# Delta rule: the inverse is turned by TensorE at each doubling level, in place of a transposed copy kept with its own products

## What is computed

```python
a_mat = jnp.where(strict, jnp.einsum('bnhid,bnhjd->bnhij', kb, kc) * decay, 0.0)
t_mat = lax.linalg.triangular_solve(a_mat, eye, left_side=True, lower=True, unit_diagonal=True)
u = jnp.einsum('bnhij,bnhjd->bnhid', t_mat, vc * bc[..., None])
w = jnp.einsum('bnhij,bnhjd->bnhid', t_mat, kb * jnp.exp(gc)[..., None])
```

## Time and profile before

| | |
|---|---|
| median of 3 runs | 2700.0 us (2696.96 to 2703.47) |
| span of the profiled execution | 2699.0 us |
| PE busy | 2646.7 us, 98% of the span |
| PEld busy | 2419.6 us, 90% |
| DVE busy | 1835.7 us, 68% |
| ACT busy | 1007.2 us, 37% |
| POOL busy | 344.1 us, 13% |
| moved by DMA | 398.75 MB, mean 148 GB/s |

### The profile page before, as it was taken

The page is one execution under the profiler, slowest core; times in us unless marked ns, Lnnn a source line. Parts: engine busy times, 40 slices in busy tenths (PEclk is TensorE's granted clock), DMA queues, the critical chain, the costliest instruction groups (busy, mean ns, idle before and its releaser), DMA issues.

```text
span 2699.0 us, 44506 instructions
## 1 busy us (share of the span) xinstructions
PE 2646.7 (98%) x17640; PEld 2419.6 (90%) x17640; DVE 1835.7 (68%) x1775; ACT 1007.2 (37%) x1045; POOL 344.1 (13%) x350
## 2 busy tenths in 40 slices
PE   8999999999999999999998999999999999999998
PEld 7999988888888987878888999999999998788886
DVE  4444545555554233548889888888888888888898
ACT  4443322222222232223354444444444444333334
POOL 5000044444442420101000000000000000000000
PEclk9999999999999999999999999999999999999999
DMA  4333222222223433679524445444544459866562
GB/s 138 102 88 91 79 79 79 82 81 78 78 78 86 109 94 117 221 268 319 187 103 133 150 161 171 155 152 148 179 148 155 151 172 305 292 205 203 175 196 104
DMA packets 345656, 398.75 MB, mean 148 GB/s; under 512 B 11481, under 2 KB 300386, under 8 KB 344418
## 3 DMA queue, kind: packets, MB, share of 16 engines
q1 hardware_dynamic: 285970, 333.30, 39.3%
q10 hardware_dynamic: 59616, 64.49, 7.0%
HBM read 325.92 MB, written 71.83 MB: 147 GB/s over the span
## 4 chain that ended last, share of the span: by engine, by line
PE 91%; DVE 2%; issue 2%; DMA 2%; ACT 1%; SPq 1%; POOL 1%; DVEq 0%; ACTq 0%; POOLq 0%
PE psum L2082 33%; PE psum L2399 10%; PE psum L2401 10%; PE psum L2400 10%; PE psum L2374 6%; PE psum L2375 6%; PE psum L2376 6%; PE psum L2242 2%; PE psum L2237 1%; DMA w_raw<-in_w_proj_a 1%; PE psum L2031 1%; PE psum L2059 1%; DMA dn_raw<-in_w_ffn_down 1%; PE psum L2221 1%; PE psum L2314 1%
## 5 line engine op out<-in xcount | busy, mean ns | idle before, releaser
L2082 PE MATMUL psum<-hn_hi,w_hi 128*128 128x264 f32 (+1 forms) x1600 | 450.7, 330 | 0.0
L2082 PE MATMUL psum<-hn_lo,w_hi 128*128 128x264 f32 (+1 forms) x1600 | 449.9, 330 | 0.0
L2082 PE MATMUL psum<-hn_hi,w_lo 128*128 128x264 f32 (+1 forms) x1600 | 449.9, 330 | 0.0
L1347 DVE TENSOR_TENSOR w_lo<-w_raw,w_hi 128x1024 fp32r<-128x1024 f32 x144 | 186.6, 1297 | 253.5 <-ACT w_hi L901 253.0
L901 ACT ACTIVATE w_hi<-w_raw 128x1024 fp32r<-128x1024 f32 x144 | 152.1, 1057 | 373.7 <-PE psum L2082 345.5
L2082 PEld LDWEIGHTS psum<-hn_lo,w_hi 128*128 128x128 f32 x1600 | 269.1, 188 | 22.7 <-issue 0.7
L2082 PEld LDWEIGHTS psum<-hn_hi,w_lo 128*128 128x128 f32 x1600 | 268.9, 188 | 22.4
L2082 PEld LDWEIGHTS psum<-hn_hi,w_hi 128*128 128x128 f32 x1600 | 269.1, 188 | 22.0 <-issue 0.2
L2374 PE MATMUL psum<-dn_hi,act_hl 128*128 128x512 f32 x616 | 240.2, 390 | 4.3 <-DVE hq L1684 2.5
L2376 PE MATMUL psum<-dn_hi,act_hl 128*128 128x512 f32 x616 | 239.8, 389 | 0.0
L2375 PE MATMUL psum<-dn_lo,act_hl 128*128 128x512 f32 x616 | 239.8, 389 | 0.0
(11 more groups left out here) (355 smaller groups left out, 6400.5 us busy)
## 6 DMA issues: line engine op xcount, KB each, us to landing
w_raw<-in_w_in SPq DMA_DIRECT2D x144, 512.0 KB, 3.9
ffn_raw<-in_w_ffn_gate SPq DMA_DIRECT2D x44, 1024.0 KB, 6.5
ffn_raw<-in_w_ffn_up SPq DMA_DIRECT2D x44, 1024.0 KB, 6.7
dn_raw<-in_w_ffn_down SPq DMA_DIRECT2D x32, 1024.0 KB, 8.3
act_hl<-act_dram SPq DMA_DIRECT2D x56, 512.0 KB, 9.0
act_dram<-comb_hi ACTq DMA_DIRECT2D x22, 896.0 KB, 4.2
act_dram<-comb_lo ACTq DMA_DIRECT2D x22, 896.0 KB, 6.2
out_raw<-in_w_out SPq DMA_DIRECT2D x16, 1024.0 KB, 9.8
```

The costliest lines, as they stand in the source:

```text
L1347: dve.tensor_tensor(wlo[s][:], raw[s][:], whi[s][:].bitcast(F32), ALU.subtract).then_inc(S["lo_ready"], 1)
L2082: ins = pe.matmul(o, lhs, r, start=kt == 0 and i == 0, stop=kt == 4 * n_chunks - 1 and i == 2)
```

## The change

V, its copy, its products and its subtractions go. At each of the first six levels, after DVE has made the new `Z`, PE turns it (four transposes of 128x128 against the identity, into bank 2), and DVE multiplies bank 2 with the mask to give the next `X`. Within a level Z's product now comes first and the turn second. The number of steps on PE and of pieces on DVE and ACT stays as it was; so does the place of the weight splits among them. POOL's program is not edited.

```diff
@@ ACT, gdn_act
-                act.wait_ge(S["x_ready"], LEVELS * v + 1)
-                act.activation(B[1][:], bank(0), ACT.Copy).then_inc(S["v_copied"], 1)
@@ DVE, gdn_dve
                 for l in range(LEVELS):
-                    if l < LEVELS - 1:
-
-                        dve.wait_ge(S["v_copied"], v + 1)
-                        dve.wait_ge(S["vx_product"], (LEVELS - 1) * v + l + 1)
-                        v_even = blocks_of(B[1][:], l, 0)
-                        dve.tensor_tensor(v_even, v_even, blocks_of(bank(2), l, 0), ALU.subtract).then_inc(S["v_ready"], 1)
-                        dve.wait_ge(S["v_ready"], (LEVELS - 1) * v + l + 1)
-                        dve.wait_ge(S["mask_ready"], LEVELS * v + l + 2)
-                        if l >= 1:
-                            dve.wait_ge(S["z_product"], LEVELS * v + l)
-                        dve.tensor_tensor(XB[(l + 1) % 2][:], B[1][:], mask_buf[(l + 1) % 2][:], ALU.mult) \
-                            .then_inc(S["x_ready"], 1)
-                        yield
                     dve.wait_ge(S["z_kept"], LEVELS * v + l + 1)
                     dve.wait_ge(S["z_product"], LEVELS * v + l + 1)
                     dve.tensor_tensor(B[11][:], kept[:], bank(1), ALU.subtract).then_inc(S["z_ready"], 1)
                     yield
+                    if l < LEVELS - 1:
+                        dve.wait_ge(S["z_turned"], (LEVELS - 1) * v + l + 1)
+                        dve.wait_ge(S["mask_ready"], LEVELS * v + l + 2)
+                        dve.tensor_tensor(XB[(l + 1) % 2][:], bank(2), mask_buf[(l + 1) % 2][:], ALU.mult) \
+                            .then_inc(S["x_ready"], 1)
+                        yield
@@ PE, gdn_pe
                     pe.wait_ge(S["x_ready"], LEVELS * v + l + 1)
                     pe.wait_ge(S["z_ready"], (LEVELS + 1) * v + l + 1)
-                    if l < LEVELS - 1:
-                        for i in range(GH):
-                            ins = pe.matmul(blocks_of(bank(2), l, 0)[:, i, :, :], B[11][:, i, :],
-                                            blocks_of(x[:], l, 0)[:, i, :, :], start=True, stop=True)
-                        ins.then_inc(S["vx_product"], 1)
-                        yield
                     for i in range(GH):
                         ins = pe.matmul(bank(1)[:, i, :], x[:, i, :], B[11][:, i, :], start=True, stop=True)
                     ins.then_inc(S["z_product"], 1)
                     yield
+                    if l < LEVELS - 1:
+                        pe.wait_ge(S["z_ready"], (LEVELS + 1) * v + l + 2)
+                        for i in range(GH):
+                            ins = pe.transpose(bank(2)[:, i, :], B[11][:, i, :], ident[:])
+                        ins.then_inc(S["z_turned"], 1)
+                        yield
```

More of the change, by code:

```diff
@@ L130 @@
 nbeg_ready beta_k_ready vb_ready kd_factor kd_ready kk_done kq_done nt_ready pt_ready s_products rhs_ready
-qs_ready n_turned z_masked z_ready z_kept z_product mask_ready x_ready v_copied v_ready vx_product vn_product
+qs_ready n_turned z_masked z_ready z_kept z_product mask_ready x_ready z_turned vn_product
 vn_ready o_product ds_product o_ready state_ready o_squared o_sum o_mean o_rms o_scaled o_turned o_stored
@@ L446, in heads_of @@
             return v.unsqueeze(2).broadcast_to([P, GH, width])
-        def blocks_of(b, l, odd):
-            return b.rearrange("p h (n two s) -> p h n two s", two=2, s=1 << l)[:, :, :, odd, :]
         def over_heads(m):
```

## The result

| | before | after |
|---|---|---|
| median of the runs | 2698.74 us (4 runs) | 2677.44 us (4 runs) |
| span of the profiled execution | 2699.0 us | 2678.8 us |

The ratio is 0.992, 95% interval 0.9907 to 0.9932: 21.3 us less by the medians, 20.2 us by the two profiled spans. The forecast was 2678 us.

What follows compares the result with a forecast made beforehand. The prediction took PE, busy almost without waits, to bound the stage. 48 cheaper steps save 21.6 us and stalls cost 0: span 2699.0 - 21.6 = 2677.4 us, median 1.0 us above, so 2678 us; range 2672 to 2687.

Steps and rivals of the forecast that it cites:

- What bounds the stage: 331 to 866 us: PE busy for 531.68 of 535 us, one wait of 3.3 us, so time taken from PE is saved.
- The price of a step: PE, 48 steps: V's product at 1.35 us replaced by a turn at 0.91; 0.45 us a step taken, 21.6 us in all.
- The turn's wait for Z: PE's turn waits for DVE's new Z, ready 0.88 us before the step is due; nothing new to pay.
- Z's product's wait for X: PE in each level: X ready 1.42 us after the turn, Z's product due at 2.29; cover 0.87 us, no stall.
- piece 11: DVE's weight split ahead of the fourth X: fits by 0.3 us; 0 taken, 0 to 5.6 us possible in seven half-chunks.
- POOL's late kept product: POOL at level 3: mask, copies and `kept` move back, cover 1.2 us; priced 0, other end 3.5 us in seven half-chunks.
- The sum: Whole kernel: span 2699.0 - 21.6 + 0 = 2677.4 us; median 1.0 us above the span, so 2678 us.
- A: Rival, every level: Z's product waits for X, the hand-off becomes the bound; 34.6 us of stall, 2713 us; chance 2%.
- C: Rival: the tight places, piece 11 and the late `kept`, stall by 5.6 and 3.5 us, 2687 us; chance 12%.
- B: Rival, PE in the levels: extra transposes let the clock fall to 1.2 GHz; 2941 us at worst; chance 2%.
- D: Rival, behind the stage: a later stage waits for a transfer and the gain is given back, 2700 us; chance 2%.
- E: Rival, PE's step: the turn costs as much as a product, 1.35 for 1.35 us, 2700 us; chance 2%.

Runs made afterwards that it cites:

- the turn as a product: The changed kernel with the turn written as an ordinary product of Z with the identity, eight instructions a step: 2700.05 us, ratio 0.9999 to the kernel before.
- the work put back: The changed kernel with a DVE subtraction after each X and ACT's copy of bank 0 once a half-chunk put back: 2678.60 us, ratio 0.9925.
- the wide version: The kernel before with V's product over all 128 columns of each head instead of 64: 2700.12 us, ratio 0.9998.
- The two late versions: The changed kernel with one or two extra 128x512 DVE operations ahead of each X: 2676.93 us (ratio 0.9915) and 2702.68 us (1.0013).
- the version without it: The changed kernel with DVE's weight split of piece 11 moved behind the next piece, the fourth X: 2678.00 us, ratio 0.9922, period 62.97 us.

## Why the prediction was right

- **What bounds the stage.** Right. PE without a wait in the rows meant that its steps are the time; the turn as a product and the work put back show it from both sides.
- **The price of a step.** Right: 1.35 us against 0.90, where 0.91 and 0.44 to 0.46 us of difference were read from the turn of N. The reading that columns don't set the price of V's product is confirmed by the wide version. The turn costs the same on Z as on N.
- **The turn's wait for Z and Z's product's wait for X.** Right at five levels of six: X 0.73 us after the turn and 0.69 us long, 0.87 us ahead of the matmuls, to the hundredth of what the rows gave. But the prediction counted the cover to the matmuls, and the weight loads, which stand behind the wait, begin 0.23 us earlier. The cover that counts is 0.64 us, and the 0.3 us that it gave piece 11 were 5.02 - 0.23 - 4.73 = 0.06. The two late versions bracket the cover between 0.61 and 1.22 us.
- **Piece 11.** Here a term was mis-sized: 0 was taken, with 0 to 5.6 us as its bounds, and the weight loads wait 3.0 us in all, of which the periods show 0.19 us a half-chunk, 1.5 us. The step that failed is the split's length: 1.59 us was taken over from the kernel before, where the split ran beside POOL's copies. It begins 2.53 us into the step (which starts at 433.00), where the rows gave 2.52, but takes 1.96 us, and X is done 5.10 us into it and not 4.73. What it runs beside had changed, though POOL's program was not edited. The copies begin 0.19 us into the step, where 0.3 was forecast, but take 1.72 us and not 3.18, so the kept product begins 2.13 us into it, 0.4 us ahead of the split. By the forecast it would have begun at about 3.7 us, behind the split's start. The prediction moved POOL's operations and kept the durations that they and the split had in other company.
- **POOL's late kept product.** Right in that nobody waits for it; wrong in the duration of the copies ahead of it, below.
- **The sum.** 21.6 us were forecast; 20.1 us come from the periods, and the difference is the 1.5 us of piece 11, by the version without it. That the median, 2677.44 us, lies within 1 us of the forecast is luck: the sum is 1.5 us off, and the four runs lie between 2675.60 and 2680.62 us.
- **The rivals.** A, the hand-off as the bound, was not so, but it lies close: two more DVE operations bring the time back to that of before. Of C a part came. B did not come: the granted clock is 1.00 over six half-chunks, each with 11 groups of four transposes where there were five. The Trainium skill, page "TensorE: Matmul & The Clock Gate", Part 4, says that the full clock does not engage for transposes; beside these gate matmuls the measurement says otherwise, and it decides. D and E fell with the time behind the last mark and with the rows of the turn.

## What to carry to other kernels

Where TensorE is without gaps, price its steps by the distances between starts. For the small products here these went with the number of instructions and not with columns: a transposition of an operand that is at hand can be cheaper than a product that updates a copy of it. Then look at what the shorter way takes away elsewhere: here the slack of an operand fell from 2.55 us to 0.87 (0.64 to the weight loads, which is where the wait stands), and one operation of another engine that ran 0.37 us longer than forecast was enough for a wait. And when a dependence moves, lay out the whole new order of an engine that was not edited, with what it runs beside, not only whether it is in time.

## What the runs showed of the hardware

- A 128x512 turn in float32 is four instructions and holds the next gate matmul for 0.35 to 0.36 us; the same turn as four products with the identity is eight and holds it for 0.80 us.
- DVE's split, which reads two tiles of SBUF, and POOL's operations lengthen each other, and the one that begins later pays. In the traces above the split is 1.22 us alone or when it begins first, and 1.77 to 1.96 us behind POOL's kept product; a small copy of 0.19 us takes 1.22 us behind the split. The kept product is 1.28 us alone and 2.19 us in the kernel before, where it begins at 446.28, behind a split of DVE (line below). The Trainium skill, page "SBUF — State Buffer", section "Who interferes with whom", says that a DVE instruction with two SBUF inputs contends with a GpSimd instruction that reads SBUF and that the order of issue decides who is held; the traces agree.

```profile
446.12 1.22 DVE L1347 TENSOR_TENSOR w_lo<-w_raw,w_hi 128x1024 fp32r<-128x1024 f32 x1
```

- POOL's three copies took 3.18 us in the kernel before and 1.72 us after, without an edit. In the changed kernel they run ahead of the split, and X no longer reads two SBUF tiles beside them. With the copies two levels later, next to a split, they take 2.71 us:

```profile
440.70 2.71 POOL L795 COPY gdn<-qkv 128x512 f32 x3
```
